# Two fused layers on one core: the second layer by token halves, its first half issued in the gather loop

## The reference

```python
def chunk(args):
    xc, ec, gc = args
    u = expert_u[ec]
    act = jax.nn.gelu(jnp.einsum('cd,ced->ce', xc, u).astype(jnp.float32))
    return jnp.einsum('ce,ced->cd', gc * act, expert_v[ec])
...
h = rmsnorm_2(x, pre_norm_w)
proj = jnp.einsum('bsd,de->bse', h, w_in)      # 1024 x 10256
o_a = moba_attention(partial_rope(heads(q_a), pos), partial_rope(heads(k_a), pos), heads(v_a))
y_a = jnp.einsum('bse,ed->bsd', o_a * jax.nn.silu(z_a), w_branch_a)
qkv = jax.nn.silu(causal_dwconv(jnp.concatenate([q_b, k_b, v_b], axis=-1), conv_w))   # 4 taps
o_b = gated_deltanet(...)                       # chunked delta rule, l2-normed q and k
y_b = jnp.einsum('bse,ed->bsd', rmsnorm_2(o_b, gdn_norm_w) * jax.nn.silu(z_b), w_branch_b)
merged = jax.nn.sigmoid(gate_a) * y_a + jax.nn.sigmoid(gate_b) * y_b
return x + rmsnorm_2(jnp.einsum('bsd,de->bse', merged, w_out), post_norm_w)
```

## Time and profile before

| | |
|---|---|
| median of 3 runs | 1384.27 us (1382.68 to 1388.41) |
| profiled execution, its own time | 1387.86 us |
| its span in the trace | 1386.1 us |
| busy: TensorE matmul / VectorE / ScalarE / GpSimd | 1141.1 / 784.2 / 451.5 / 274.7 us |
| moved by DMA | 378.16 MB, mean 273 GB/s |
| granted TensorE clock, mean over the span | 0.929 |

### The profile page before, as it was taken

The page is one execution under the profiler, slowest core; times in us unless marked ns, Lnnn a source line. Parts: engine busy times, 40 slices in busy tenths (PEclk is TensorE's granted clock), DMA queues, the critical chain, the costliest instruction groups (busy, mean ns, idle before and its releaser), DMA issues.

```text
span 1386.1 us, 15226 instructions
## 1 busy us (share of the span) xinstructions
PE 1141.1 (82%) x5688; PEld 666.4 (48%) x5688; DVE 784.2 (57%) x1899; ACT 451.5 (33%) x1269; POOL 274.7 (20%) x261
## 2 busy tenths in 40 slices
PE   6979995877887776768986656669998998999997
PEld 2867672432243223112221111124787887899883
DVE  5474656887855999555454444440387666732111
ACT  1122212645432434335333333330234543223101
POOL 0000002433343444433443333300000000000000
PEclk9977976988888899999999999989999999999999
DMA  9995506998999999999999999924423131114130
GB/s 393 327 361 212 197 0 229 346 346 350 398 401 423 420 402 411 418 422 422 421 420 422 422 421 422 421 111 184 187 118 122 61 122 61 68 65 175 65 118 30
DMA packets 56949, 378.16 MB, mean 273 GB/s; under 512 B 7171, under 2 KB 10412, under 8 KB 11820
## 3 DMA queue, kind: packets, MB, share of 16 engines
q0 software_dynamic: 36864, 268.45, 47.5%
q1 hardware_dynamic: 19344, 106.71, 20.1%
q10 hardware_dynamic: 668, 2.04, 0.4%
HBM read 376.12 MB, written 1.06 MB: 272 GB/s over the span
## 4 chain that ended last, share of the span: by engine, by line
PE 48%; DMA 22%; DVE 20%; ACT 5%; issue 3%; POOL 1%; ACTq 0%; SPq 0%; POOLq 0%; DVEq 0%
DMA AR<-in_puv,idx 20%; PE ps L592 19%; PE ps L896 7%; PE ps L600 7%; DVE AR L1623 6%; PE ps L1064 3%; DMA W<-in_w_mod 2%; PE ps L814 2%; DVE AR L1742 2%; PE ps L842 2%; ACT acc L2070 1%; POOL AR L2471 1%; PE ps L761 1%; DMA X<-in_x 1%; ACT av L2187 1%
## 5 line engine op out<-in xcount | busy, mean ns | idle before, releaser
L896 PE MATMUL ps<-AR,acc 128*64 128x512 f32 x912 | 354.5, 678 | 164.9 <-ACT acc L2070 162.8
L2471 POOL DMA_INDIRECT AR<-in_puv,idx x256 | 274.4, 1072 | 628.4 <-PE ps L896 373.2
L592 PE MATMUL ps<-hT,W 128*128 128x256 f32 x1216 | 282.9, 391 | 12.6 <-DVE AR L1347 8.2
L896 PEld LDWEIGHTS ps<-AR,acc 128*64 128x64 f32 x912 | 82.7, 145 | 409.0 <-ACT acc L2070 327.8
L592 PEld LDWEIGHTS ps<-hT,W 128*128 128x128 f32 x1216 | 235.9, 197 | 50.4 <-DVE AR L1347 9.1
L1623 DVE CUSTOM_DVE_ANT_0 AR<-AR,mixT 128x1024 f32<-128x1024 f32 x128 | 156.7, 1225 | 150.8 <-DMA AR<-in_puv,idx 150.8
L1623 DVE CUSTOM_DVE_ANT_0 AR<-AR,tok 128x1024 f32<-128x1024 f32 x128 | 153.3, 1221 | 60.2 <-DMA AR<-in_puv,idx 59.9
L2185 ACT ACTIVATE av<-av 128x1 f32<-128x1 f32 x256 | 51.3, 201 | 306.6 <-DVE av L1623 306.4
L2070 ACT ACTIVATE acc<-fold,av 128x64 f32<-128x64 f32 x228 | 79.3, 348 | 7.4
L2187 ACT ACTIVATE av<-av,gwp 128x1 f32<-128x1 f32 x256 | 75.4, 294 | 8.3
L600 PE MATMUL ps<-W,hT 128*128 128x512 f32 (+3 forms) x224 | 67.8, 461 | 0.0
(11 more groups left out here) (350 smaller groups left out, 1288.2 us busy)
## 6 DMA issues: line engine op xcount, KB each, us to landing
W<-in_w_in SPq DMA_DIRECT2D x50, 1024.0 KB, 6.9
W<-in_w_mod SPq DMA_DIRECT2D x24, 1024.0 KB, 11.2
W<-in_w_out SPq DMA_DIRECT2D x4, 1024.0 KB, 6.0
W<-in_wq SPq DMA_DIRECT2D x4, 1024.0 KB, 7.3
AR<-in_puv,idx POOLq DMA_INDIRECT x256, 11.3
W<-in_wba SPq DMA_DIRECT2D x4, 1024.0 KB, 6.0
W<-in_wbb SPq DMA_DIRECT2D x4, 1024.0 KB, 5.8
W<-in_wo SPq DMA_DIRECT2D x4, 1024.0 KB, 6.0
```

Source lines behind the costliest of these rows:

```text
L592: t = mm(b[:, o:o + S], slab(i)[:, k, c:c + P], src[:, k, :], start=(k == 0), stop=(k == 7))
L896: t = mm(of(("E", a, c))[64 * g:64 * g + 64, :], dg_at((2 * p + g) % NDG, late), GB[:, places[g], D + c * 512:D + c * 512 + 512], start=(m ...
L2471: eng.indirect_dma_start(GB[:, n, :], None, puv, bass.IndirectOffsetOnAxis(ap=idx[:, a, c:c + 1], axis=0)).then_inc(*gp.dma(f"g{n}", "gat" ...
```

## The change

`combine` is split into `weight` (ScalarE: gelu, gate, scaled identity) and `accumulate` (TensorE: the four matmuls), both put at the same place as before, behind the two dots of their own pair. For a = 1, `accumulate` waits for both identities of its pair before its first matmul.

The second layer is written as `second_chores(a)` for one half of 128 tokens. The chores for a = 0 (104 projection pieces of two matmuls of 512 columns, and 114 others) are dealt out over the 64 turns 64 to 127, by a cost of 1.75 a piece and 0.9 or less for the others, 3.94 a turn, behind `accumulate`. The chores for a = 1 come after the loop. Every projection keeps 128 tokens in the array and streams 512 columns (`proj`), so that the results lie with tokens on partitions; where channels are wanted there, four transposes (`turned`) and a ScalarE copy follow. Each of the 26 slabs is therefore loaded twice, into a ring of three slots (the fourth keeps k and v). SyncE loads slab i + 3 when the projection of slab i is done.

The convolution (`conv_turn`) works on 4 heads by 128 tokens: four products with broadcast weights and three additions, of 512 elements each. `l2_scale` takes the reciprocal of 128x512 elements, twice for each group of 4 heads. The inverse has one group of 4 heads at a time. Sigmoid and silu are made from tanh.

```diff
+SLABS += 2 * [({"ba": "wba", "bb": "wbb", "o": "wo2"}.get(key, "w_in2"), COLUMN[key] + 512 * n, 512) for key, n in ORDER]
+RING = (2, 0, 1)
...
+def slot_of(i):
+    return i % NSLOT if i < FRONT else RING[(i - FRONT) % 3]
...
+PIECE, HOP, SPREAD = 1.75, 0.9, 65.0
...
+    def proj(key, n, *between, k0=0, k1=8):
+
+        for q, k in enumerate(range(k0, k1, 2)):
+            do("proj", key, n, k, k + 2, cost=PIECE)
+            if k == 6:
+                do(*taken(key, n), cost=0)
+            for chore in between[q] if q < len(between) else ():
+                do(*chore, cost=0 if chore[0] in ("conv_silu", "l2_scale") else HOP)
...
+    proj((0, 0), 0, [], [("ms", 0)])
+    proj((1, 0), 0, [("decay_sum",)], [("conv_turn", 0, 0), ("mt", 0)], two * [("ms", 1)])
+    do("conv_silu", 0, 0, cost=0)
...
+    proj("ba", 0, hops[6:7], hops[7:8], hops[8:9], hops[9:10])
...
-        do("combine", p, places, bool(state["late"]))
+        do("weight", p, bool(state["late"]))
+        do("accumulate", p, places, bool(state["late"]))
...
-        if p >= 63 and spread == 2 and x2 is None:
-            x2 = x2_steps(0)
-        if p >= 64 and x2 is not None:
-            advance(x2, 1)
-            if ("x2_norm", 0) in out and not hb:
-                do("norm_h", 0)
-                hb = True
-        if hb and qk < 16:
-            do("qk_piece", "qk"[(qk // 4) % 2], qk // 8, 2 * (qk % 4))
-            qk += 1
-        elif qk == 16:
-            qk += 1
-            do("rope", "q", 0)
-            do("rope", "k", 0)
-    assert qk == 17
+        if a:
+            assert spread == 2
+            spent += share
+            while rest and spent > 0:
+                cost, chore = rest.pop(0)
+                spent -= cost
+                do(*chore)
+    last = second_chores(1)
+    while rest or last:
+        for _ in range(2):
+            if rest:
+                do(*rest.pop(0)[1])
+        if last and (not rest or last[0][1][0][:2] == "x2"):
+            do(*last.pop(0)[1])
...
-            def combine(p, places, late):
+            def accumulate(p, places, late):
+                if a:
+                    pe.wait_ge(("dg", p, 0), ("dg", p, 1))
...
+            def turned(use, tiles, ready, frees):
+
+                b, old = take(use, frees)
+                pe.wait_ge(*old, *ready)
+                for q in range(4):
+                    t = tr(b[:, q * P:q * P + P], tiles[q], ident)
+                return t
...
+            def proj(a, key, n, k0, k1):
+                use, i = ("proj", a, key, n), slab_of(a, key, n)
                 if k0 == 0:
-                    b, old = take(("rot", kind, 0, n))
...
+            def conv_turn(a, j, n):
+                turned(("craw", a, j, n), [rawt[a][:, q * P:q * P + P] for q in range(4)], [("rawt", a, (j, n), n)],
+                       ("raw", a, j, n)).then_inc(*pe.sig("craw_mm", a, j, n))
...
-            def conv2(c):
-                kind, hd = c // 8, c % 8
-                dst = vT[:, hd, :] if kind == 2 else qk[:, hd, 1 - kind, :]
-                wc = [PV[:, V_CW2 + u * 24 + c:V_CW2 + u * 24 + c + 1] for u in range(4)]
-                ve.wait_ge(("raw", c), ("acc", 127, 1))
-                t = link(ts(dst, raw[:, c % 4, 0:256], wc[0], None, MUL))
...
-                    ins = stt(dst, raw[:, c % 4, u:u + 256], wc[u], dst, MUL, ADD)
...
+                def tap(o, u):
+                    w = PV[:, V_CW2 + u * 24 + c:V_CW2 + u * 24 + c + 4].unsqueeze(2).to_broadcast([P, 4, P])
+                    return tt(o, src[:, :, u:u + P], w, MUL)
...
+                t = link(tap(dst, 0))
                 for u in range(1, 4):
+                    if u > 1:
+                        ve.wait_ge(t)
+                    t2 = link(tap(tmp, u))
+                    ve.wait_ge(t, t2)
+                    ins = tt(dst, dst, tmp, ADD)
...
+            def conv_silu(a, j, n):
+
+                dst = conv_to(a, j, n)
+                ve.wait_ge(("tanh", a, j, n))
+                stt(dst, heads(th[a]), 1.0, dst, ADD, MUL).then_inc(*ve.sig("silu", a, j, n))
+                if j < 2:
...
+            def l2_scale(a, n):
+                for j in range(2):
+                    r, o = rt[a][:, j, :], qk[a, n][:, :, 1 - j, :]
+                    ve.wait_ge(("l2_root", a, j, n))
+                    t = link(rec(r, r))
+                    ve.wait_ge(t)
+                    stt(o, o, (0.5 * DK, 0.5)[j], heads(r), MUL, MUL).then_inc(*ve.sig(("l2_q", "l2_k")[j], a, n))
...
+            def inv_x(a, l, g):
+                if l < 6:
+                    masked(a, l + 1, g)
...
-            def combine(p, places, late):
+            def weight(p, late):
...
+            def raw_out(a, j, n):
+                ac.wait_ge(("proj", a, (j, n), n))
...
+                copy(rawt[a], of("proj", a, (j, n), n)[:, :], "rawt", a, (j, n), n)
+
+            def conv_turn(a, j, n):
+                ac.wait_ge(("craw_mm", a, j, n), ("x2_gate", 1, 1) if a else ("halo", 0))
...
+                if (j, n) != (0, 0):
+                    ac.wait_ge(("conv2", a, *((j - 1, n) if j else (2, 0))))
+                copy(raw[a][:, :, 3:P + 3], bank4("craw", a, j, n), "raw", a, j, n)
+
...
+                elif chore == "proj" and what[4] == 8:
+                    a, key, n = what[:3]
+                    if slab_of(a, key, n) + 3 < len(SLABS):
+                        load(slab_of(a, key, n) + 3, ("proj", a, key, n))
```

More of the change, by code:

```diff
@@ L327, in loop_chores @@
     h1, h2, second, spread = half1(pair), 0, False, 0
-    x2, hb, qk = None, False, 0
+    rest = second_chores(0)
+    share, spent = sum(cost for cost, _ in rest) / SPREAD, 0.0
     for p in range(P):
@@ new lines, in rope_turn, with beta @@
+            def rope_turn(a, kind, n):
+                turned(("rt", kind, a, n), [rot[kind, a][:, (4 * n + q) * P:(4 * n + q) * P + P] for q in range(4)],
+                       [("roped", kind, a, n)], ("ropeT", kind, a, n)).then_inc(*pe.sig("rope_mm", kind, a, n))
+            def beta(a):
+                b, old = take(("bd", a), ("dt", a), ("beta_tanh", a))
+                pe.wait_ge(*old, "bdw")
+                for k in range(8):
+                    pe.wait_ge(hb(a, k))
+                    t = mm(b[:, 0:16], hb_T[a][:, k, :], bdw[:, k, :], start=(k == 0), stop=(k == 7))
+                t.then_inc(*pe.sig("bd_mm", a))
@@ L1710, in decay @@
                 ve.wait_ge(t)
[L1711 removed]
+                t = link(rec(t1(2), t1(2)))
                 ve.wait_ge(t)
[L1713 removed]
+                t = link(tt(t1(2), t1(2), t1(1), MUL))
                 ve.wait_ge(t)
[L1715 removed]
+                t = link(tt(t1(3), t1(2), t1(2), MUL))
                 ve.wait_ge(t)
[L1717 removed]
+                t = link(ts(t1(4), t1(3), 1.0 / 17, None, MUL))
@@ new lines, in conv_silu, with l2_scale @@
+            def conv_silu(a, j, n):
+                ac.wait_ge(("conv2", a, j, n))
+                act(heads(th[a]), conv_to(a, j, n), ACT.Tanh, scale=0.5).then_inc(*ac.sig("tanh", a, j, n))
+            def l2_scale(a, n):
+                for j in range(2):
+                    ac.wait_ge(("l2_mm", a, j, n), *([("l2_k", a, 0), ("l2_q", a, 0)] if n else [("x2_gain", 0, 1)]))
+                    act(rt[a][:, j, :], of("l2", a, j, n)[:, :], ACT.Sqrt, scale=0.25, bias=eps).then_inc(*ac.sig("l2_root", a, j, n))
@@ L2527, in sync @@
                     load_keys(1, ("tp_mm", 6, 1))
-                elif chore == "load_row":
-                    load_row(*what, ("keys_mm", 1, 3) if what[0] else ("tp_mm", 7, 1))
-                elif chore == "attn_mm" and what[3] == 8:
-                    load(22 + what[1], ("o_mm", 1, what[1]))
+                elif chore == "load_row" and what[0] == 0:
+                    load_row(0, ("rows", 0, 0), ("tp_mm", 7, 1))
+                elif chore == "attn_mm" and what[1] == 0 and what[3] == 8:
+                    load(FRONT, ("o_mm", 1, 0))
```

1382 lines of the change are left out of this document (584 added, 798 removed).

## The result

The change takes 1582.16 us (median of 5 runs, 1581.76 to 1589.84), the kernel before 1383.24 (5 runs, 1378.21 to 1388.41): a ratio of 1.1459, 95% interval 1.1424 to 1.1493. It is slower by 14.6%, not by the 8% of the forecast, and 22 us above the range's upper end. The profiled execution took 1589.84 us, its span is 1588.0; it lies 7.7 us above the median, and a stretch of it set beside that of another run can be off by as much. One execution of experiment 10 (2012.81 us) and one of the kernel before on that chip (1876.65) fell in a slower state and are left out of every comparison.

A forecast was written before the change was run, and what follows sets the result against it. Before, gather DMA bounds turns 64 to 127 and TensorE the tail; after, a serial chain bounds the turns. Start 595.8, turns 590 and tail 308 give a span of 1493.8, so 1492 us; range 1415 to 1560.

The forecast's parts named there:

- the chain: Turns 64 to 127: dots, weight, sums, TensorE's chore, copy, VectorE's chore, next dots run serially; 590 us, 9.2 a turn.
- Rivals A: Turns 64 to 127: chain hidden, gathers bound, turns take the DMA's 462 us; total 1364, 1.5% faster; chance 0.10.
- B: Turns 64 to 127: chain half hidden, 8 us a turn, 512 in all; total 1414; chance 0.13 with what lies near.
- D: Rival for the whole kernel: nothing moves; held excluded by the order of instructions; no chance of its own given.
- light turn: One of 16 turns with projection pieces alone and no chain: TensorE's 5.5 us each, sum 88.
- `l2_scale`: Two turns with silu, two scalings and two reciprocals of 128x512 at 3.3 us each: 14.1 us a turn, 28 in all.
- Dots, weight, sums: Base of the turns' price, the three one after the other: 2.5 + 1.0 + 1.95 = 5.4 us.
- rival C: Turns 64 to 127: table loads on the chain, weight delayed, TensorE at times 1.2 GHz; 650 us, total 1552; chance 0.07 with beyond.
- Table loads: ScalarE's 20 function-set loads in the turns fall in idle time: 0 of 26 us taken, 26 kept for the upper end.
- Inversion turns: 17 turns with a piece, a quarter of the groups' matmuls, a copy and a subtraction: 9.2 us each, sum 156.
- The tail: Behind the last dot, a = 1: entry 25, TensorE's work 242, stalls 34, end 7; 308 us where 471 stood.
- DMA: 462 us for gathers and slabs: DMA limit of turns 64 to 127: gathers 319 us plus 26 slabs 143, under the 590 forecast for the turns.

The follow-up runs named there:

- experiment 10: The change with tanh in place of exponentials and roots in a = 0's second layer, leaving ScalarE 2 of 20 table loads in turns 64 to 127: 1573.77 us.
- experiments 1: The change with the sums of pair p issued behind the dots of pair p + 1, ahead of that turn's chores: 1393.53 us, ratio 1.0055.
- experiment 6: The change with the sums behind the chores in their own turn (dots, weight, chores, sums) in turns 64 to 127: 1387.90 us, ratio 1.0011.
- Experiment 3: The change with three matmuls that lead nowhere added ahead of the wait for the identities in turns 65 to 127: 1558.37 us, ratio 1.1262.
- Experiment 2: The change without the wait for both identities ahead of the first sum, each sum waiting for its own: 1545.26 us, ratio 1.1147.
- experiment 4: The change with three dead-end matmuls ahead of the sums and without the wait for both identities: 1544.60 us, ratio 1.1164.

## Why the prediction was right in kind and short in size

- **What bounds before, and the chain: right.** The traces show the forecast order of waits in turn 86, and experiments 1 and 6 undo it by moving four matmuls a turn, worth 189 and 194 us. Rivals A and B (chain hidden or half hidden) are refuted, as is D. The sums of turn 78 start 5.5 us before those of turn 79, as forecast for a light turn (67 and 74: 6.9 and 7.0), and those of 105 start 13.4 us before those of 106 (forecast: near 14).
- **`l2_scale`: the right number by luck.** Its turns, priced at 14.1, took 13.9 us both times (826.06 to 839.96 for turn 88). But the price held the sums, and with the sums behind the chores (experiment 6) both turns take 13.9 us too: behind the dots stand a tanh, a table load of 1.28 us and a root on ScalarE, then VectorE's reciprocals. The load, priced at nothing, counts in turn 110, which takes 12.7 us without it (experiment 10); turn 88 stays at 13.9 there, since its second root waits for a matmul behind the sums.
- **The step that failed: "Dots, weight, sums [...] are 2.5 + 1.0 + 1.95 = 5.4 us".** The 1.95 came from a row of a kernel whose TensorE was seldom idle for long. The very chain that I forecast makes it idle for 3 to 7 us ahead of the sums, and then they take up to 3.68. It is a term mis-sized by 0.99 us (2.97 - 1.98), 64 times: 63 us, if each lies on the path, of the 74 that the turns are too long. The pieces behind them start slow too (2.94 us in some rows for two matmuls, where the earlier trace rows had 1.98). Experiment 3 shows the cause: the clock back to 0.95, 48 us less of sums, and 33 us less in the turns in spite of added work. That it accounts for all of the 74 is not shown. I had this as a part of rival C, with a chance of 0.07 (650 us for the turns; measured 664), though it follows from the forecast itself and should have stood in the sum. The Trainium skill, "TensorE: Matmul & The Clock Gate", section "HAM oscillation — how this bites in real kernels", describes this pattern for waits (there for DMA) that return with every tile, each followed by work at the slow level; the trace agrees for waits on other engines, with 3.68 against 1.94 us.
- **The joint wait** wasn't in the sum. Experiment 2 gives 37 us for it, experiment 4 only 14 with the clock held, so the two terms overlap and must not be added.
- **Table loads: "0 of the 26".** The count of 20 was right; experiment 10 shows that 8 to 10 us of 23 count; turns 104 and 110 show two ways in which they get onto the path. Behind no load does the trace show a drain: 1001.75 + 1.28 = 1003.03, and the function starts at 1003.05; in 11 of the 20 cases it starts within 0.07 us of the load's end.
- **Inversion turns:** forecast 9.2 us, measured 10.7 in turns 92 to 100 (875.91 to 972.55) and 10.8 in 113 to 121, again the sums.
- **The tail: 308 forecast, 333 measured.** TensorE is busy for 275 us, where I had 242 and the four pieces of 7. The trace divides the 26 us: when the last dot ends, TensorE still has eight pieces of a = 0 ahead, not four (7 us more), and the sums of two pairs (4); the tail's 224 projection matmuls take 214 us, 0.957 each in place of 0.866 (20); the other work is some 5 us under the forecast. The clock is 0.93 there, not the 0.98 of the earlier trace rows; that it makes the 0.957 was not tested. The idle time, 333 - 275 = 58, is near the forecast's (entry without the pieces 18, stalls 34, end 7: 59).
- **DMA: 462 us for gathers and slabs, right.** Without the chain, 455 us of it show in the turns (0.96 x 473). This also shows why even a good order gains nothing: in experiment 6 the turns grow by 473 - 319 = 154 us, 136 of them DMA (455 - 319) and the rest DMA standing still, and the tail falls by 471 - 319 = 152.

## What to carry to other kernels

When several engines walk one list, work that waits for a long chain (here the sums) belongs behind the work that is ready, or each turn becomes the sum of its engines' times; one place in the order was worth 14%. A chain that you forecast also forecasts idle time on TensorE: price the matmuls behind it at the low clock, from a row with such an idle time ahead of it. Before you move work under a loop that DMA bounds, count the bytes that it brings along: here the best orders ended within 1% of the kernel before.

## What the runs showed of the hardware

Adding 189 matmuls without a use made the kernel 24 us faster, by the clock (0.82 to 0.95 in the turns). The sums of eight records took 1.94 us behind an idle time of 2.90 us and 3.33 and 3.68 behind 4.12 and 3.31: the last idle stretch alone does not set the level. And a reciprocal of 128x512 took 3.35 us on VectorE, nearly five times a product's 0.69.
